# Head slots of a hybrid decoder block: the scores of a coming step are issued before the output projection's tile, not behind it

## The chip, the cores and the metric

One NeuronCore of a Trainium2 chip runs the whole kernel. The metric is the device time of one execution in microseconds (us), taken as the median of several runs. Everything is computed in 32-bit floating point; a matrix product is made of three matmuls on operands split into a high and a low part (hi x hi, lo x hi, hi x lo).

## What is computed

One layer of a decoder block over 512 tokens of width 1024: a projection that feeds an RG-LRU group and an attention group of 8 heads, an output projection of both groups together, a gated MLP with a short convolution, and a gated per-layer embedding. The part that matters here, cut from the reference:

```
proj = u @ w_in[i]
x_lru, g_lru, q, k, v = jnp.split(proj, split_at, axis=-1)
...
y_lru = rglru(...) * jax.nn.gelu(g_lru)
y_att = moba_attention(q, k, v, slopes)
h = h + jnp.concatenate([y_lru, y_att], axis=-1) @ w_out[i]
```

With 512 tokens there are two key blocks of 256 and the top-3 choice takes every past block, so each head is causal attention with a distance penalty: scores, softmax, probabilities times values. The matrix `w_out` has a half for the LRU rows and a half for the attention rows.

## The kernel before, in words

Each engine has its own hand-written, in-order list of instructions; semaphores tie them. TensorE (PE) does all matmuls, VectorE (DVE) and ScalarE (ACT) the element-wise work, GpSimd (POOL) mostly the low parts of weights. Weights stream in chunks of 128 x 1024 through a ring of four buffers.

The change lies in the stretch where the heads are worked. Three things are woven there on PE:

- **scores(st)**, one for each of 8 steps (lines 1151 to 1169): 12 matmuls on 64 rows (10 rows of the timeline, since two kinds are merged there), which write the banks 4, 5 and 6 of PSUM. These three banks exist once, so from step 1 on line 1155 has PE wait until all four parts of `logits(st-1)` have been read out of them by DVE (`logit_ok`).
- **turn_probs(h)** (lines 1171 to 1185): 10 transposes of the probabilities of head h into banks 0 to 2; then **values(h-1)** (lines 1187 to 1200): 8 matmuls into bank 7. In head 0 there are no values yet.
- **out_lru(h)** (lines 1202 to 1219): 12 matmuls, one of the eight output tiles of the LRU half of `w_out`. They are recorded under the lines 1040 to 1042 of the helper `three`. From h = 2 on they write bank 3, so they wait for the tile before to have been added (`part_ok`).

Ahead of the head loop PE issues `scores(0), out_lru(0), scores(1), out_lru(1), scores(2), out_lru(2)`. Then slot h of the loop is `turn_probs(h)`, `values(h-1)`, a projection tile, `scores(h+3)`. The projection tile is `out_lru(h+3)` in the slots 0 to 4; in the slots 5 to 7, where there are no scores left to issue, it is a part of the attention half (`out_att`).

The other two engines have slots of their own:

- DVE, slot h (lines 922 to 934): `add_lru(h+2)` (line 888, waits for the end of `out_lru(h+2)`), `logits(h+2)` (line 867, four parts, waits for `scores(h+2)`), the low parts of the turned probabilities of h (`prTlo`, line 929), `add_values(h-1)` (line 920), `normalise(h+2)` (lines 874 and 880, waits for the exponentials).
- ACT, slot h (lines 564 to 577): the high parts of the turned probabilities (`prThi`, line 569), `move_values(h-1)` (line 553, waits for `values(h-1)`), `exps(h+2)` (line 527, each part waits for its logits), in even slots `hi_att`, and `top_scale(h+2)` (line 536, waits for the reciprocals of `normalise`).

`turn_probs(h)` waits for the probabilities of both steps of its pair of heads: in an even slot, h = 2, 4, 6, that is the `top_scale(h+1)` which ACT issued in the slot before.

POOL splits the chunks of the attention half of `w_out` (lines 349 to 364) between the slots; each waits for `chunk_done`, which the odd tiles of `out_lru` raise.

Of the kernel before, what the change touches and what calls it, by code (L numbers as in the profile page):

```python
# [80 lines left out]
def score_order():  # L81

    halves = (((3, 4, 0), (0, 6, 0)), ((1, 6, P), (2, 5, 0)))
    order = []
    for half, tiles in enumerate(halves):
        start = 0
        for i, b, c0 in tiles:
            for term in range(3):
                order.append((start, half, term, i, b, c0))
                start += (i + 1) * P  # L90
    return [step[1:] for step in sorted(order)]


STEPS = 2 * PAIRS
# [17 lines left out]
def build(nc, x, x_t, p_t, lead_in, weights, vectors, gates, out):  # L112
    with ExitStack() as ctx:
# [80 lines left out]
        def parts_upto(st):  # L194

            return sum(len(parts(i)) for i in range(st))
# [177 lines left out]
        def _(act):  # L374
# [147 lines left out]
            def exps(st):  # L522

                for n, (e, i, _, _) in enumerate(parts(st)):
                    v = prob[(2 * (st // 2) + e) % 4][:, S_OFF[i]:S_OFF[i] + (i + 1) * P]
                    act.wait_ge(logit_ok, parts_upto(st) + n + 1)
                    nc.scalar.activation(v, v, ACT.Exp, bias=sm[:, st % 2, n:n + 1], scale=-1.0,
                                         accum_out=sm[:, st % 2, 10 + n:11 + n]).then_inc(exp_ok, 1)

            def top_scale(st):  # L530

                act.wait_ge(rinv_ok, st + 1)
                for n, (e, i, _, _) in enumerate(parts(st)):
                    if i >= TT - 2:
                        v = prob[(2 * (st // 2) + e) % 4][:, S_OFF[i]:S_OFF[i] + (i + 1) * P]
                        nc.scalar.activation(v, v, ACT.Copy, scale=sm[:, st % 2, 15 + n:16 + n]).then_inc(top_ok, 1)
# [27 lines left out]
            for h in range(HEADS):  # L564
                for part, (c0, b, w, _) in enumerate(TURNED):
                    act.wait_ge(pt_done, 3 * h + part + 1)
                    if h >= 2 and part == 0:
                        act.wait_ge(pv_done, h - 1)
                    nc.scalar.activation(prThi[h % 2][:, c0:c0 + w], bank[b][:, 0:w], ACT.Copy).then_inc(prT_hi, 1)
                if h:  # L570
                    move_values(h - 1)
                if h + 2 < STEPS:
                    exps(h + 2)
                if h and h % 2 == 0:
                    hi_att(h // 2 - 1)
                if h + 2 < STEPS:
                    top_scale(h + 2)
# [457 lines left out]
        def _(pe):  # L1035
# [115 lines left out]
            def scores(st):  # L1151

                p = st // 2
                if st:
                    pe.wait_ge(logit_ok, parts_upto(st))
                    pe.wait_ge(qkT_lo, PAIRS + p + 1)
                for half, term, i, b, c0 in score_order():
                    if st == 0 and term == 0:
                        pe.wait_ge(qkT_lo, PAIRS + b - 3)
                    e = half if st % 2 == 0 else 1 - half  # L1160
                    r, w = slice(DH * e, DH * (e + 1)), (i + 1) * P
                    q = (qkThi, qkTlo, qkThi)[term][0][r, p, i * P:w]
                    k = (qkThi, qkThi, qkTlo)[term][1][r, p, 0:w]
                    if i == 0 and term == 0:
                        pe.wait_ge(s_mid, st + 1)
                    last = mm(bank[b][:, c0:c0 + w], q, k, start=term == 0, stop=term == 2)  # L1166
                    if i == 1 and term == 2:
                        last.then_inc(s_mid, 1)
                last.then_inc(s_done, 1)

            def turn_probs(h):

                pe.wait_ge(prob_ok, 4 * (h // 2 + 1))
                pe.wait_ge(top_ok, 4 * (h // 2 + 1))
                if h:
                    pe.wait_ge(prT_lo, 3 * h)
                else:
                    pe.wait_ge(part_ok, 1)
                for c0, b, _, key_tiles in TURNED:
                    for kt in key_tiles:  # L1180
                        for i in range(kt, TT):
                            src = prob[h % 4][:, S_OFF[i] + kt * P:S_OFF[i] + (kt + 1) * P]
                            at_ = PT_OFF[kt] - c0 + (i - kt) * P
                            last = nc.tensor.transpose(bank[b][:, at_:at_ + P], src, ident[:, :])  # L1184
                    last.then_inc(pt_done, 1)

            def values(h):

                pe.wait_ge(prT_lo, 3 * (h + 1))
                if h:  # L1190
                    pe.wait_ge(att_ok, h)
                else:
                    pe.wait_ge(part_ok, 2)
                for kt in range(TT):
                    w = T - kt * P
                    v = vs[:, kt, h, :]
                    for n, src in enumerate((prThi[h % 2], prTlo[h % 2])):
                        last = mm(bank[PV_BANK][:, kt * P:T], v, src[:, PT_OFF[kt]:PT_OFF[kt] + w],  # L1198
                                  start=kt == 0 and n == 0, stop=kt == TT - 1 and n == 1)
                last.then_inc(pv_done, 1)  # L1200

            def out_lru(h):

                c, s = C_OL + h // 2, h // 2
                pe.wait_ge(w_lo, c - (RING - 1))
                pe.wait_ge(y_lo, LT)
                if h == 0:
                    pe.wait_ge(v_lo, 1)
                elif h == 1:
                    pe.wait_ge(qkT_lo, 2 * PAIRS)  # L1210
                elif h == 2:
                    pe.wait_ge(v_lo, TT)
                else:
                    pe.wait_ge(part_ok, h)
                for k in range(LT):
                    w = slice(k * 2 * P + (h % 2) * P, k * 2 * P + (h % 2 + 1) * P)
                    last = three(bank[FILL_BANK[h]][:, :], whi[s][:, w], wlo[s][:, w], mixhi[:, k, :], mixlo[:, k, :],
                                 k == 0, k == LT - 1)
                last.then_inc((half_done, chunk_done)[h % 2], 1)

            def out_att(s, tiles):

                pe.wait_ge(w_lo, C_OA + s - (RING - 1))
                for k, half in sorted(((k, half) for k in tiles for half in range(2)), key=lambda o: (o[0] // 2, o[1])):
                    if k == 0 and (s, half) in ((0, 0), (0, 1), (2, 0), (3, 0)):

                        pe.wait_ge(*{(0, 0): (part_ok, KD), (0, 1): (logit_ok, 4 * HEADS), (2, 0): (prT_lo, 3 * HEADS),
                                     (3, 0): (att_ok, HEADS)}[s, half])
                    pe.wait_ge(att_lo, k + 1)
                    w = slice(k * 2 * P + half * P, k * 2 * P + (half + 1) * P)  # L1230
                    last = three(bank[OA_BANK[2 * s + half]][:, :], whi[s][:, w], wlo[s][:, w],
                                 mixhi[:, LT + k, :], mixlo[:, LT + k, :], k == 0, k == PAIRS - 1)
                if tiles[-1] == PAIRS - 1:
                    last.then_inc(chunk_done, 1)
# [5 lines left out]
            for h in range(HEADS):  # L1240
                turn_probs(h)
                if h:
                    values(h - 1)
                if h + 3 < KD:
                    out_lru(h + 3)
                elif h == 5:
                    out_att(0, (0, 1))
                    out_att(1, (0,))
                elif h == 6:
                    out_att(1, (1,))  # L1250
                else:
                    out_att(0, (2,))
                    out_att(1, (2,))
                if h + 3 < STEPS:
                    scores(h + 3)
            values(HEADS - 1)
            out_att(2, (0, 1, 2))
            out_att(0, (3,))
# [139 lines left out]
```

## Times and profile before

| what | value |
|---|---|
| median of 3 runs | 656.53 us |
| lowest and highest of them | 656.22 and 656.76 us |
| the profiled execution's own time | 654.96 us |
| its span, first to last instruction | 653.2 us |
| mean granted clock of TensorE | 0.999 |
| PE busy (matmuls) | 646.2 us, 99% of the span |
| DVE busy | 354.2 us |
| ACT busy | 292.9 us |
| POOL busy | 326.8 us |

How to read it: the profile is one execution; times in the trace count from its first instruction. A timeline row gives the start, the time from there to the end of the last instruction of the row, the engine, the line, the operation, the tiles, how many instructions are merged in it, and in brackets how long the engine had been idle before it and what ended that. Matmuls are pipelined, so rows of PE overlap, and the distance between two starts says more than a duration. The same holds for rows of DVE and ACT, which overlap by some 0.07 us to 0.1 us. "issue" as a releaser means that the profile saw no event that ended the idle time.

### The profile page before, as it was taken

How to read it: one execution, taken by the hardware profiler on the slowest of the kernel's cores; microseconds unless marked ns; L12 is line 12 of the kernel's file. 1: busy time of each engine (PE TensorE's matmuls, PEld its weight loads, DVE VectorE, ACT ScalarE, POOL GpSimd, SP SyncE). 2: the span in 40 equal slices, each digit the busy share in tenths (PEclk: the TensorE clock that was granted, in tenths of full speed). 3: DMA queues.
4: the chain of work that ended last, by engine and by line, in shares of the span. 5: the costliest groups of instructions: out<-in, count | busy, mean ns of one | idle time of the engine just before them, and what ended most of it. 6: DMA issues, size and time to landing. Idle time of an engine off the chain costs nothing.

```text
span 653.2 us, 8651 instructions
## 1 busy us (share of the span) xinstructions
PE 646.2 (99%) x2980; PEld 535.0 (82%) x2980; DVE 354.2 (54%) x491; ACT 292.9 (45%) x445; POOL 326.8 (50%) x239
## 2 busy tenths in 40 slices
PE   8999999999999999999999999999999999999997
PEld 7788888887888888888888888888888888888886
DVE  4583699977649676555555555555422222222464
ACT  6668653778736454333333333333322222223521
POOL 6673433742207377555555555555544444444430
PEclk9999999999999999999999999999999999999999
DMA  8732221210403233222222222222322222222211
GB/s 319 276 125 91 97 96 65 96 34 1 162 1 125 70 100 126 96 96 96 96 96 96 96 96 96 96 96 96 102 97 96 99 95 97 96 98 97 75 64 50
DMA packets 20039, 65.41 MB, mean 100 GB/s; under 512 B 2224, under 2 KB 2864, under 8 KB 20016
## 3 DMA queue, kind: packets, MB, share of 16 engines
q1 hardware_dynamic: 19872, 64.97, 29.1%
q8 instruction: 14, 0.23, 0.1%
q10 hardware_dynamic: 144, 0.14, 0.1%
q14 instruction: 9, 0.07, 0.0%
HBM read 63.00 MB, written 2.10 MB: 100 GB/s over the span
## 4 chain that ended last, share of the span: by engine, by line
PE 98%; DMA 1%; DVE 0%; ACT 0%; issue 0%; DVEq 0%
PE bank L1040 30%; PE bank L1042 30%; PE bank L1041 30%; PE bank L1166 2%; PE bank L1198 2%; PE bank L1184 1%; PE bank L1078 1%; PE bank L1086 1%; PE bank L1081 1%; DMA lead<-in_lead_in 1%; PE bank L1136 1%; PE bank L1331 0%; PE bank L1277 0%; PE bank L1104 0%; ACT uhi L394 0%
## 5 line engine op out<-in xcount | busy, mean ns | idle before, releaser
L324 POOL TENSOR_TENSOR wlo<-raw,whi 128x512 fp32r<-128x512 f32 x106 | 142.9, 1348 | 262.9 <-ACT whi L382 262.5
L382 ACT ACTIVATE whi<-raw 128x1024 fp32r<-128x1024 f32 x102 | 107.6, 1058 | 226.1 <-PE bank L1042 226.0
L1040 PE MATMUL bank<-uhi,whi 128*128 128x512 f32 (+1 forms) x496 | 192.6, 388 | 0.0
L1042 PE MATMUL bank<-uhi,wlo 128*128 128x512 f32 (+1 forms) x496 | 191.4, 386 | 0.0
L1041 PE MATMUL bank<-ulo,whi 128*128 128x512 f32 (+1 forms) x496 | 191.4, 386 | 0.0
L325 POOL TENSOR_TENSOR wlo<-raw,whi 128x512 fp32r<-128x512 f32 x106 | 164.3, 1550 | 0.0
L1040 PEld LDWEIGHTS bank<-uhi,whi 128*128 128x128 f32 x496 | 93.2, 188 | 19.6 <-issue 0.7
L1041 PEld LDWEIGHTS bank<-ulo,whi 128*128 128x128 f32 x496 | 93.2, 188 | 19.5 <-issue 0.7
L1042 PEld LDWEIGHTS bank<-uhi,wlo 128*128 128x128 f32 x496 | 93.2, 188 | 18.6
L974 DVE SCALAR_TENSOR_TENSOR tmp<-tmp,vec 128x511 f32<-128x511 f32 (+1 forms) x48 | 63.4, 1320 | 27.9 <-ACT tmp L614 24.8
L1042 PE MATMUL bank<-acthi,wlo 128*128 128x512 f32 x192 | 74.7, 389 | 0.0
L1041 PE MATMUL bank<-actlo,whi 128*128 128x512 f32 x192 | 74.7, 389 | 0.0
L1040 PE MATMUL bank<-acthi,whi 128*128 128x512 f32 x192 | 74.7, 389 | 0.0
L992 DVE TENSOR_TENSOR res<-res,bank 128x512 f32 x8 | 5.5, 687 | 92.3 <-PE bank L1042 92.3
L1040 PEld LDWEIGHTS bank<-acthi,whi 128*128 128x128 f32 x192 | 36.0, 188 | 7.5
L1042 PEld LDWEIGHTS bank<-acthi,wlo 128*128 128x128 f32 x192 | 36.0, 188 | 7.4
L1041 PEld LDWEIGHTS bank<-actlo,whi 128*128 128x128 f32 x192 | 36.0, 188 | 7.4
L981 DVE TENSOR_TENSOR tmp<-tmp 128x512 f32<-128x512 f32 x24 | 27.0, 1124 | 22.3 <-ACT tmp L619 22.0
L1040 PE MATMUL bank<-whi,uhi 128*128 128x512 f32 x96 | 37.5, 391 | 0.0
L1042 PE MATMUL bank<-whi,ulo 128*128 128x512 f32 x96 | 37.4, 389 | 0.0
L1041 PE MATMUL bank<-wlo,uhi 128*128 128x512 f32 x96 | 37.4, 389 | 0.0
L983 DVE TENSOR_TENSOR actlo<-tmp,acthi 128x512 f32 (+1 forms) x24 | 19.0, 792 | 21.3 <-ACT acthi L623 21.3
(190 smaller groups left out, 823.8 us busy)
## 6 DMA issues: line engine op xcount, KB each, us to landing
raw<-in_weights SPq DMA_DIRECT2D x106, 512.0 KB, 3.3
res<-in_x_t SPq DMA_DIRECT2D x8, 256.0 KB, 5.4
xtok<-in_x SPq DMA_DIRECT2D x4, 512.0 KB, 8.1
raw<-in_weights SPq DMA_DIRECT2D x7, 256.0 KB, 6.4
out<-fin SPq DMA_DIRECT2D x7, 256.0 KB, 2.0
gw<-in_gates SPq DMA_DIRECT2D x1, 512.0 KB, 11.2
ptok<-in_p_t SPq DMA_DIRECT2D x1, 512.0 KB, 3.6
out<-fin SPq DMA_DIRECT2D x2, 128.0 KB, 1.8
```

What stands on the lines that cost most here:

```text
L324: nc.gpsimd.tensor_tensor(wlo[s][:, 0:CW // 2], raw[s][:, 0:CW // 2], whi[s][:, 0:CW // 2].bitcast(F32), ALU.subtract)
L325: nc.gpsimd.tensor_tensor(wlo[s][:, CW // 2:CW], raw[s][:, CW // 2:CW], whi[s][:, CW // 2:CW].bitcast(F32), ALU.subtract).then_inc(w_lo, 1)
L382: nc.scalar.activation(whi[s][:, :], raw[s][:, :], ACT.Copy).then_inc(w_hi, 1)
L974: V.scalar_tensor_tensor(y[:, k:T], g[:, 0:T - k], vec[:, bass.ds(f + (V_FCW + (2 - k) * FT), 1)], y[:, k:T], ALU.mult, ALU.add).then_inc( ...
L981: V.tensor_tensor(y, g, y, ALU.mult).then_inc(f_prod, 1)
L983: V.tensor_tensor(actlo[:, f, :], y, acthi[:, f, :].bitcast(F32), ALU.subtract).then_inc(act_lo, 1)
L1040: mm(o, ahi, bhi, start=start, stop=False)
L1041: mm(o, ahi, blo, start=False, stop=False)
L1042: return mm(o, alo, bhi, start=False, stop=stop)
L1078: mm(bank[m][:, :], whi[s][:, w[m]], uhi[:, k, :], start=k == 0, stop=False)
L1166: last = mm(bank[b][:, c0:c0 + w], q, k, start=term == 0, stop=term == 2)
L1198: last = mm(bank[PV_BANK][:, kt * P:T], v, src[:, PT_OFF[kt]:PT_OFF[kt] + w], start=kt == 0 and n == 0, stop=kt == TT - 1 and n == 1)
```

## The change

In each of the slots 0 to 4, `scores(h+3)` moves on PE from behind `out_lru(h+3)` to ahead of it. No instruction is added or removed, no wait is changed, and the lists of DVE, ACT, POOL and SyncE stay as they are. The loop ahead of the slots (steps 0 to 2) keeps its order, and the slots 5 to 7 issue no scores.

```
@@ -1241,6 +1241,8 @@
                 turn_probs(h)
                 if h:
                     values(h - 1)
+                if h + 3 < STEPS:
+                    scores(h + 3)
                 if h + 3 < KD:
                     out_lru(h + 3)
                 elif h == 5:
@@ -1251,8 +1253,6 @@
                 else:
                     out_att(0, (2,))
                     out_att(1, (2,))
-                if h + 3 < STEPS:
-                    scores(h + 3)
             values(HEADS - 1)
```

## Rows read from the trace of the kernel before

**Rows 1.** The page: busy time of the engines, granted clock, chain that ended last.

```profile
PE 646.2 (99%) x2980; PEld 535.0 (82%) x2980; DVE 354.2 (54%) x491; ACT 292.9 (45%) x445; POOL 326.8 (50%) x239
...
PEclk9999999999999999999999999999999999999999
...
PE 98%; DMA 1%; DVE 0%; ACT 0%; issue 0%; DVEq 0%
```

**Rows 2.** Timeline of PE, slot 0 (start us, us, engine, line, operation, tiles).

```profile
137.60 0.40 PE L1042 MATMUL bank<-mixhi,wlo 128*128 128x512 f32 x1
137.84 1.26 PE L1184 MATMUL bank<-ident,prob 128*128 128x128 f32 x10
138.88 0.47 PE L1040 MATMUL bank<-mixhi,whi 128*128 128x512 f32 x1
...
141.48 0.39 PE L1042 MATMUL bank<-mixhi,wlo 128*128 128x512 f32 x1
141.80 0.50 PE L1166 MATMUL bank<-kThi,qThi 64*128 64x512 f32 x2
...
143.07 1.31 PE L1184 MATMUL bank<-ident,prob 128*128 128x128 f32 x10
```

**Rows 3.** Timeline of PE, slot 1, from the values to the scores.

```profile
144.14 0.48 PE L1198 MATMUL bank<-prThi,vs 128*128 128x512 f32 x1
...
145.44 0.45 PE L1040 MATMUL bank<-mixhi,whi 128*128 128x512 f32 x1
...
148.02 0.39 PE L1042 MATMUL bank<-mixhi,wlo 128*128 128x512 f32 x1
148.34 0.49 PE L1166 MATMUL bank<-kThi,qThi 64*128 64x512 f32 x2
```

**Rows 4.** Timeline of PE: the transposes that open the slots 2 to 6.

```profile
149.99 1.28 PE L1184 MATMUL bank<-ident,prob 128*128 128x128 f32 x10 [0.31 <-issue]
...
156.52 1.31 PE L1184 MATMUL bank<-ident,prob 128*128 128x128 f32 x10
...
163.44 1.28 PE L1184 MATMUL bank<-ident,prob 128*128 128x128 f32 x10 [0.32 <-issue]
...
169.95 1.31 PE L1184 MATMUL bank<-ident,prob 128*128 128x128 f32 x10
...
176.88 1.28 PE L1184 MATMUL bank<-ident,prob 128*128 128x128 f32 x10 [0.23 <-issue]
```

**Rows 5.** Timeline of DVE, slot 0: the added tile and the logits.

```profile
138.04 0.69 DVE L888 TENSOR_TENSOR res<-res,bank 128x512 f32<-128x512 f32 x1 [2.86 <-PE bank L1042]
138.65 0.68 DVE L867 CUSTOM_DVE_ANT_0 prob<-bank,dist 128x512 f32<-128x512 f32 x1
...
140.08 0.28 DVE L867 CUSTOM_DVE_ANT_0 prob<-bank,dist 128x128 f32<-128x128 f32 x1
140.29 0.08 DVE L867 DVE_READ_ACCUMULATOR2_ANT sm<- 128x1 f32 x1
```

**Rows 6.** Timeline of PE: scores of step 2 and the projection tile behind them.

```profile
133.71 0.49 PE L1166 MATMUL bank<-kThi,qThi 64*128 64x512 f32 x2
...
134.98 0.50 PE L1040 MATMUL bank<-mixhi,whi 128*128 128x512 f32 x1
```

**Rows 7.** Timeline of ACT, slot 1: the moved values, the first exponential, the scaling.

```profile
145.64 0.60 ACT L553 ACTIVATE tmp<-bank 64x512 f32<-64x512 f32 x1 [0.51 <-PE bank L1198]
146.14 0.71 ACT L527 ACTIVATE prob<-prob,sm 128x512 f32<-128x512 f32 x1
...
148.66 1.23 ACT L536 ACTIVATE prob<-prob,sm 128x512 f32<-128x512 f32 x2 [0.24 <-DVE sm L874]
```

**Rows 8.** Timeline of DVE, slot 1: low parts of the turned probabilities, the reciprocals.

```profile
144.95 1.61 DVE L929 TENSOR_TENSOR prTlo<-bank,prThi 128x512 fp32r<-128x512 f32 x3
...
148.45 0.18 DVE L874 RECIPROCAL sm<-sm 128x4 f32<-128x4 f32 x1 [1.30 <-ACT prob L527]
```

**Rows 9.** Timeline of POOL: the second attention chunk of `w_out`.

```profile
142.86 1.04 POOL L352 CAST whi<-raw 128x1024 fp32r<-128x1024 f32 x1 [3.97 <-DVE prob L880]
```

## Prediction: the chances of a swap on a full engine

> **What bounds the kernel now.** I read the page first: TensorE is busy for 99% of the span at its full granted clock (the 2.4 GHz level), and the chain that ended last is 98% PE [rows 1]. So the time is PE's list of matmuls plus its idle gaps. A swap on PE leaves the list as it is, and can only make or remove gaps. Next I read PE's timeline through the slots for the brackets: ahead of the transposes of the slots 2, 4 and 6 PE idles 0.31, 0.32 and 0.23 us [rows 4]; the slots 0, 1, 3 and 5 open without a gap. There is thus some 0.9 us to win in the heads at the very most, and any new wait costs its full length. The swap shortens the time between two instructions that depend on each other through DVE, so the third view is DVE's timeline, which shows when the logits leave the score banks.
>
> **The dependence.** scores(h+3) waits until all four parts of logits(h+2) are read. On DVE logits(h+2) stand behind add_lru(h+2), which waits for the end of out_lru(h+2). Before, out_lru(h+2) ran ahead of scores(h+2): the tile was added while the scores ran, and from scores(h+2) to scores(h+3) PE had the transposes, the values and a whole tile to do. After, out_lru(h+2) is the last thing in PE's slot, so add_lru starts only when the next slot opens, the logits follow it, and PE has only transposes and values (in slot 0 only transposes) to cover both.
>
> **Slot 0, the main term.** Nothing ahead of it is changed: scores(2), out_lru(2) and the transposes at 137.84 stay [rows 2, 6]. DVE is already in the new pattern here: add_lru(2) starts at 138.04, the logits at 138.65, and their last part ends at 140.29 + 0.08 = 140.37 [rows 5]. The transposes take 138.88 - 137.84 = 1.04 us to the next matmul [rows 2]; scores start 0.32 us behind the last matmul of a tile where transposes start 0.24 us behind it (148.02 to 148.34, 137.60 to 137.84), 0.08 more, so free scores(3) would start at 138.96 [rows 2, 3]. How long PE takes from the release to the first matmul isn't shown for DVE as releaser. The nearest row: ACT's scaling ends at 148.66 + 1.23 = 149.89 and the transposes that wait for it start at 149.99, 0.10 us [rows 4, 7]. The other end is DVE starting 0.04 us after PE's last matmul ended (137.60 + 0.40 to 138.04) [rows 2, 5]; upwards I allow 0.3, three times the row. I take 0.10 as it has PE as the waiter. So scores(3) start at 140.47: a gap of 1.51 us. Behind them: scores to tile 134.98 - 133.71 = 1.27, tile to transposes 137.84 - 134.98 = 2.86 [rows 2, 6]. Slot 1 opens at 140.47 + 1.27 + 2.86 = 144.60 in place of 143.07: **+1.53 us** (+1.47 to +1.73).
>
> **Slots 1 and 3.** Call t the start of the slot's transposes. DVE repeats slot 0: logits done at t + 140.37 - 137.84 = t + 2.53, scores may start at t + 2.63. PE free: transposes 1.07 (143.07 to 144.14), values 1.30 (144.14 to 145.44), 0.08 for the change to scores: t + 2.45 [rows 2, 3]. A new gap of 0.18. Without other waits the slot would take 2.63 + 1.27 + 2.86 = 6.76 us. But the slot's end waits for top_scale: from 143.07 to 149.99 it took 6.92, and slot 3 6.92 too (156.52 to 163.44) [rows 2, 4]. That chain runs on ACT from the values: moved at 145.64, exponentials at 146.14 = t + 3.07, reciprocals, scaling [rows 7, 8]. Its logits were wanted at t + 3.07 and are there at t + 2.53, so it is neither later nor earlier, and 6.92 hides 6.76. **+0** each (0 to +0.18).
>
> **Slots 2 and 4.** They open 0.16 later than the tile ahead of them ended (6.92 - 6.76), and so DVE, which had started with that tile, has the logits out at t + 2.37 and PE may go at t + 2.47; free it would go at t + 2.45. The slot takes 2.47 + 1.27 + 2.86 = 6.60, in place of 6.53 (149.99 to 156.52) and 6.51 (163.44 to 169.95) [rows 4]. **+0.07 and +0.09** (0 to +0.25 each).
>
> **Slot 5 and on.** No scores are issued. add_lru(7) and the logits come some 0.4 us later against the transposes than before, but the exponentials again wait for the values, t + 3.07 against t + 2.53; the slot stays at 176.88 - 169.95 = 6.93 us [rows 4]. I count 0.
>
> **What is moved along.** prTlo(h) on DVE went ahead from 144.95 = t + 1.88 and now follows the logits at t + 2.45; it ends at about t + 4.05, adding the values at t + 4.7, and the reciprocals wait for ACT until 148.45 = t + 5.38 anyway [rows 8], so ACT and the next slot see none of it. The projection's ends move, and with them the DVE add (free by then) and POOL: the cast of the second attention chunk waited for the probabilities until 142.86 [rows 9] and will now wait for the end of out_lru(3) at about 144.8; with its two splits (2.5 us more by its own pace) it is ready before 149, and the first attention tile isn't issued before slot 5, after 170 [rows 4]. The swap passes no DMA issue and no other queue. After the heads everything is shifted as a block, and I find no gap of PE there that could take the shift in.
>
> **Sum.** 1.53 + 0.07 + 0.09 = +1.69 us. The profiled execution took 654.96, so its counterpart would be 656.65; the median of the runs lies 1.57 above the profiled time, and I set the sum on the median: 656.53 + 1.69 = **658.2 us**, +0.26%. What a measurement of this kernel can tell from no change is about 0.2%, 1.31 us, so the forecast lies just past that line, and the lower half of its error crosses it.
>
> **The rivals.**
>
> *The gap is taken in by the waits that are there.* If the three top_scale waits ended at fixed times, set by ACT alone, the later PE would find them over: 149.99 less the free start of slot 2, which is 148.34 + 1.27 = 149.61, gives 0.38 for each of the first two and 0.23 to 0.4 for the third, some 1.1 us [rows 3, 4, 6]. The result would be 1.69 - 1.1 = +0.6, 657.1 us, not slower by over 0.2%. It decides if ACT's exponentials could start ahead of the moved values. Against it: ACT's bracket at 145.64 says that it waited for PE's values [rows 7], so the chain moves with PE. Chance 0.09.
>
> *Every slot pays.* If the release of the scores, or the later prTlo, reaches ACT's chain as well, the four slots 1 to 4 pay 0.18 each on top of what they have, without the cover of the 6.92: 1.53 + 4 x 0.18 + 0.16 = +2.4, 658.9 us. For it: a part of DVE's slack, t + 4.7 against t + 5.38, is used up. Against: 0.7 us of it is left. Chance 0.09.
>
> *The swap brings what its order suggests.* Scores that end sooner could give earlier logits, exponentials and scaling, and two of the waits (0.38 each) would vanish: without the gap in slot 0 -0.8, 655.7. It needs DVE's logits to be free of the tile; they are not, by DVE's own order. Chance 0.02, half of it past 0.2% for what I don't see.
>
> *The clock falls.* PE has a gap of 1.5 us in slot 0 where it had none, and if the granted clock then drops to 1.2 GHz for about a slot, its 6.5 us of matmuls take twice the time: +1.7 + 6.5, 664.7 us. Against it: the page shows the clock at its top in every slice, also in the first, in which PE began with nothing done [rows 1]. Chance 0.03. The Trainium skill ("TensorE: Matmul & The Clock Gate", "The HAM clock gate") says that idle time gates the clock down to half and that renewed activity releases it; the trace of before has no gap of such length inside the stream of matmuls that could show it, so the rule stays as this rival and no more.
>
> **How the numbers follow.** The forecast's own case has 0.77: 0.69 of it lands above +1.31 us, 0.08 below, as the runs alone spread by 0.5 us. Faster: 0.01 (half of the third rival). Same: 0.08 + 0.09 + 0.01 = 0.18. Slower: 0.69 + 0.09 + 0.03 = 0.81. The range: down to +0.9 (gap of 1.47, no term behind it, half the spread of the runs and a rest), 657.4, up to +2.7, 659.2, which takes in "every slot pays"; left out are the first rival, the third and the clock, and a tail of the forecast, about 2 in 10.
>
> **What the profile after would show.** Right: an idle bracket of about 1.3 to 1.5 us ahead of the scores in slot 0, ended by DVE's logits; DVE's add_lru in the slots 1 to 4 starting 0.2 us after the transposes, the logits right behind; the slots 1, 3 and 5 still 6.9 us long, the slots 2 and 4 6.6; granted clock unchanged. Wrong: slot 0 no longer than 5.3 us, slots 1 and 3 over 7.0, brackets ahead of slots 2, 4 and 6 that are gone, or a clock below the top behind slot 0.

## The result, and the profile after

| | before | changed |
|---|---|---|
| median | 656.09 us (10 runs, 655.43 to 656.76) | 657.54 us (10 runs, 657.08 to 658.55) |
| the profiled execution | 654.96 us | 657.29 us |
| its span | 653.2 us | 655.5 us |
| start of the transposes of slot 0 | 137.84 us | 138.57 us |
| PE busy | 646.2 us | 646.2 us |

The ratio of the times is 1.0022, 95% interval 1.0014 to 1.0031: 1.45 us slower, between 0.9 and 2.0. The value on record was 658.2 us, +1.69 us. Of the 0.66 us between 658.2 and 657.54, 0.44 us is the median of before that the sum was set on (656.53, three runs, where ten give 656.09). One run of the kernel before, of the 81 that stood beside the experiments, took 810.75 us at a mean granted clock of 0.753; it is left out of all comparisons.

PE did the same work in both, so the loss is idle time. The waits of PE in the profile of the changed kernel (who waited for whom: us in total, times, longest):

```profile
...
PE bank L1166 <- DVE sm L867: 1.3, 1, 1.3
PE bank L1040 <- DVE ulo L675: 1.3, 1, 1.3
...
PE bank L1184 <- issue: 0.2, 1, 0.2
```

The first line shown is the predicted gap, ahead of the scores (L1166), ended by DVE's logits (L867). The second lies at 23.29 us, 115 us ahead of the heads: PE waits there for low parts that DVE computes (L675). The profile of before has no such line, so the stretch ahead of the change differs from execution to execution. In the thirteen profiles of this study the transposes of slot 0 start between 137.84 and 139.63 us, whatever the kernel. The two spans differ by 2.3 us; 0.73 of it lies ahead of the slots, so spans must not be compared, slots must. From the transposes of slot 0 to those of slot 6 the old kernel takes 39.04 us and the new one 40.57, **+1.53**; from there to the end 476.32 and 476.36.

Timeline of PE in the changed kernel, slots 0 and 1, which answers to [rows 2, 3]:

```profile
138.57 1.25 PE L1184 MATMUL bank<-ident,prob 128*128 128x128 f32 x10
141.16 0.49 PE L1166 MATMUL bank<-kThi,qThi 64*128 64x512 f32 x2 [1.33 <-DVE sm L867]
...
145.32 1.25 PE L1184 MATMUL bank<-ident,prob 128*128 128x128 f32 x10
...
147.91 0.49 PE L1166 MATMUL bank<-kThi,qThi 64*128 64x512 f32 x2
```

Timeline of DVE, the same stretch, which answers to [rows 5]:

```profile
138.77 0.69 DVE L888 TENSOR_TENSOR res<-res,bank 128x512 f32<-128x512 f32 x1 [2.86 <-PE bank L1042]
139.38 0.68 DVE L867 CUSTOM_DVE_ANT_0 prob<-bank,dist 128x512 f32<-128x512 f32 x1
...
141.02 0.08 DVE L867 DVE_READ_ACCUMULATOR2_ANT sm<- 128x1 f32 x1
...
145.52 0.69 DVE L888 TENSOR_TENSOR res<-res,bank 128x512 f32<-128x512 f32 x1 [1.99 <-PE bank L1042]
...
147.77 0.08 DVE L867 DVE_READ_ACCUMULATOR2_ANT sm<- 128x1 f32 x1
```

Read them together. In slot 0 the tile is added at 138.77, the logits end at 141.02 + 0.08 = 141.10, and the scores start at 141.16. In slot 1 DVE has itself become idle for 1.99 us until the tile is done (before, it started its add in that slot at 142.71 without a bracket, ahead of the transposes at 143.07), adds it at 145.52, and its logits end at 147.85, 0.06 us ahead of the scores at 147.91: the pair runs hand in hand, as in slot 0, but values now cover most of it. What is left of the gap shows in the distance from the last matmul of the values to the scores, in slot 1 and in slot 2:

```profile
147.53 0.27 PE L1198 MATMUL bank<-prTlo,vs 128*128 128x128 f32 x1
147.91 0.49 PE L1166 MATMUL bank<-kThi,qThi 64*128 64x512 f32 x2
...
154.45 0.27 PE L1198 MATMUL bank<-prTlo,vs 128*128 128x128 f32 x1
154.65 0.49 PE L1166 MATMUL bank<-kThi,qThi 64*128 64x512 f32 x2
```

In slot 1 it is 0.38 us, in slot 2 it is 0.20; the 0.18 between them is the wait of slot 1, as long as predicted. The starts of the transposes of the later slots, which answer to [rows 4]:

```profile
152.20 1.28 PE L1184 MATMUL bank<-ident,prob 128*128 128x128 f32 x10
...
158.82 1.26 PE L1184 MATMUL bank<-ident,prob 128*128 128x128 f32 x10
...
165.69 1.28 PE L1184 MATMUL bank<-ident,prob 128*128 128x128 f32 x10
...
172.28 1.25 PE L1184 MATMUL bank<-ident,prob 128*128 128x128 f32 x10
...
179.14 1.28 PE L1184 MATMUL bank<-ident,prob 128*128 128x128 f32 x10 [0.23 <-issue]
```

The brackets ahead of slots 2 and 4 are gone, but the slots ahead of them are not shorter for it: the gap has moved to the scores in the middle of the slot, and the slot still ends where ACT's scaling ends. Behind the last matmul of the tile (151.80) the transposes come after 0.40 us, where they come after 0.23 us when nothing holds them (145.09 to 145.32). ACT in slot 1, which answers to [rows 7]:

```profile
147.85 0.59 ACT L553 ACTIVATE tmp<-bank 64x512 f32<-64x512 f32 x1 [0.53 <-PE bank L1198]
148.34 0.71 ACT L527 ACTIVATE prob<-prob,sm 128x512 f32<-128x512 f32 x1
...
150.87 1.23 ACT L536 ACTIVATE prob<-prob,sm 128x512 f32<-128x512 f32 x2 [0.25 <-DVE sm L874]
```

The scaling ends at 150.87 + 1.23 = 152.10 and the transposes follow at 152.20, 0.10 behind as before.

### The profile page after: what moved, and what is told of

It reads as the page before. It is cut to its first block, busy times and chain, and to the rows that moved or that the text cites. A ratio compares the mean times of both kernels' runs of the same rounds, so it can differ in the third digit from the quotient of the medians.

```text
span 655.5 us, 8651 instructions
## 1 busy us (share of the span) xinstructions
PE 646.2 (99%) x2980; PEld 534.8 (82%) x2980; DVE 354.9 (54%) x491; ACT 293.0 (45%) x445; POOL 326.7 (50%) x239
## 4 chain that ended last, share of the span: by engine, by line
PE 95%; DVE 2%; DMA 1%; SPq 1%; ACT 1%; issue 0%; DVEq 0%
PE bank L1040 30%; PE bank L1042 30%; PE bank L1041 30%; PE bank L1166 2%; PE bank L1198 1%; DMA res<-in_x_t 1%; PE bank L1184 1%; DVE prob L867 1%; PE bank L1136 1%; DVE small L704 0%; SPq L253 0%; DVE ulo L675 0%; DVE res L888 0%; ACT uhi L394 0%; SPq L260 0%
```

## The experiments

All kernels ran beside runs of the kernel before. Lengths of slots are distances between the starts of the transposes in the profile, in us; they are free of the differing start of the kernel, and so resolve a tenth where the medians don't.

| kernel | slot 0 | 1 | 2 | 3 | 4 | 5 | sum | ratio of times (95%) |
|---|---|---|---|---|---|---|---|---|
| before | 5.23 | 6.92 | 6.53 | 6.92 | 6.51 | 6.93 | 39.04 | |
| changed | 6.75 | 6.88 | 6.62 | 6.87 | 6.59 | 6.86 | 40.57 | 1.0022 (1.0014 to 1.0031) |
| swap in slot 0 alone | 6.73 | 6.87 | 6.53 | 6.92 | 6.51 | 6.93 | 40.49 | 1.0021 (1.0012 to 1.0031) |
| swap in slots 1 to 4 | 5.25 | 6.92 | 6.54 | 6.87 | 6.57 | 6.88 | 39.03 | 1.0003 (0.9994 to 1.0012) |
| swap, logits first on DVE | 5.32 | 6.88 | 6.57 | 6.87 | 6.54 | 6.87 | 39.05 | 0.9996 (0.9987 to 1.0005) |
| logits first, no swap | 5.21 | 6.93 | 6.59 | 6.93 | 6.64 | 6.93 | 39.23 | 1.0007 (0.9998 to 1.0016) |
| one op added, no swap | 5.22 | 6.93 | 6.50 | 6.93 | 6.51 | 6.93 | 39.02 | 1.0003 (0.9994 to 1.0012) |
| two ops added, no swap | 5.52 | 6.91 | 6.51 | 6.92 | 6.52 | 6.92 | 39.30 | 1.0004 (0.9994 to 1.0014) |
| swap, small op added | 7.09 | 6.88 | 6.58 | 6.87 | 6.58 | 6.87 | 40.87 | 1.0032 (1.0020 to 1.0045) |
| swap, one op added | 8.89 | 6.88 | 6.57 | 6.87 | 6.58 | 6.87 | 42.66 | 1.0056 (1.0043 to 1.0069) |
| swap, two ops added | 10.81 | 6.87 | 6.61 | 6.87 | 6.58 | 6.87 | 44.61 | 1.0078 (1.0062 to 1.0095) |
| exponentials early, no swap | 5.25 | 6.54 | 6.53 | 6.55 | 6.53 | 6.54 | 37.94 | 0.9979 (0.9971 to 0.9988) |
| all three orders changed | 5.33 | 6.56 | 6.54 | 6.56 | 6.56 | 6.49 | 38.04 | 0.9990 (0.9981 to 0.9998) |

**Which slots pay?** The swap was cut in two.

```
# slot 0 alone: (0,); its complement: (1, 2, 3, 4)
+                if h in (0,):
+                    scores(h + 3)
                 if h + 3 < KD:
                     out_lru(h + 3)
...
-                if h + 3 < STEPS:
+                if h + 3 < STEPS and h not in (0,):
                     scores(h + 3)
```

> The kernel before with the swap made in slot 0 alone; the slots 1 to 4 keep tile, then scores. Theory (the tile's add stands ahead of the logits on DVE, and slot 0 has no values to cover both): nearly the whole loss sits here, a bracket of 1.3 to 1.5 us ahead of the scores of slot 0, slot 0 6.75 us long in place of 5.23, all other slots as before; +1.5 us against the kernel before. Rival (each swapped slot costs its share, by the change of order on PE itself): a fifth of the loss, +0.3 us.

> The kernel before with the swap made in the slots 1 to 4 and not in slot 0. Theory: slot 0 as before (5.23 us); slots 1, 3 and 5 unchanged within 0.1 us since their end is set by ACT's scaling, slots 2 and 4 longer by 0.07 to 0.09: between 0 and +0.2 us in all, no change that can be measured. Rival (each slot costs its share): four fifths of the loss, +1.2 us.

Measured: slot 0 alone gives 657.70 us against 655.85 and a slot 0 of 6.73 us; the other four give 656.01 and a sum of slots that is 0.01 below before. The whole loss is in slot 0, where there are no values to cover the logits; slot 1 is 0.05 shorter. The rival of equal shares falls. In the second kernel slots 2 and 4 are 0.01 and 0.06 longer, as forecast or less, and slots 3 and 5 give 0.05 each back.

**What makes PE wait: the swap, or DVE's order?** The same swap, with the logits ahead of the tile's add:

```
@@ DVE, slot h
-                if h + 2 < KD:
-                    add_lru(h + 2)
                 if h + 2 < STEPS:
                     logits(h + 2)
+                if h + 2 < KD:
+                    add_lru(h + 2)
```

> The changed kernel with one more edit, on DVE: in each slot the logits stand ahead of the tile's add. Theory: the scores' wait is for logits that no longer wait for the tile; in slot 0 the logits are out near turn start minus 1 us, the bracket ahead of the scores of slot 0 is gone, slot 0 is back at 5.2 to 5.3 us, slots 1, 3, 5 stay at 6.9 and slots 2 and 4 at 6.55: equal to the kernel before within 0.2 us. Rival (scores next to the values or transposes cost PE by themselves): still +1 us or more. A second rival (earlier logits bring earlier exponentials): up to 0.8 us faster than before; theory says no, as ACT's exponentials stand behind the moved values.

Measured: 655.88 us, no difference from before, slot 0 back at 5.32. DVE's timeline of this kernel around its slot 0:

```profile
136.80 0.69 DVE L867 CUSTOM_DVE_ANT_0 prob<-bank,dist 128x512 f32<-128x512 f32 x1
...
138.45 0.08 DVE L867 DVE_READ_ACCUMULATOR2_ANT sm<- 128x1 f32 x1
139.75 0.69 DVE L888 TENSOR_TENSOR res<-res,bank 128x512 f32<-128x512 f32 x1 [1.22 <-PE bank L1042]
```

and PE's:

```profile
139.55 1.26 PE L1184 MATMUL bank<-ident,prob 128*128 128x128 f32 x10
140.73 0.50 PE L1166 MATMUL bank<-kThi,qThi 64*128 64x512 f32 x2
```

The logits are out at 138.53, a microsecond ahead of the transposes, and the scores have no bracket. So the wait came from the tile's add in front of the logits, not from the scores' new neighbours on PE. A rest of 0.09 us in slot 0 (5.32 against 5.23) is the order on PE itself: from the transposes to the scores it takes 1.18 us (139.55 to 140.73) with nothing waiting, where it took 1.04 to the tile. It also shows that the earlier scores bring nothing of their own.

The DVE edit alone, without the swap:

> The kernel before with the DVE edit alone: logits ahead of the tile's add, no swap on PE. It splits the pair: theory expects no change, within 0.2 us, as the logits then start when the scores end, at the same time as now (0.6 us earlier in the odd slots at most) and nobody waits for them sooner. If DVE's order by itself gains or costs, it shows here.

Measured: 656.52 us, ratio 1.0007, not clear of 1; but the sum of slots is 0.19 longer, all in slots 2 and 4; the expectation had named no cause for that. In the old order the tile comes before the scores on PE, and it waits for the add of the tile before it (they share bank 3). In slot 1 of this kernel, the add on DVE, then the last row of values and the first of the tile on PE:

```profile
146.40 0.68 DVE L888 TENSOR_TENSOR res<-res,bank 128x512 f32<-128x512 f32 x1
...
146.91 0.28 PE L1198 MATMUL bank<-prTlo,vs 128*128 128x128 f32 x1
147.23 0.47 PE L1040 MATMUL bank<-mixhi,whi 128*128 128x512 f32 x1
```

They are 0.32 apart where nobody waits at 0.11 (145.33 to 145.44 in the kernel before); the add had ended at 147.08. In the odd slots ACT's scaling hides this; in the slots 2 and 4 the two rows are 0.19 and 0.20 apart (153.81 to 154.00 in slot 2, with the add's end at 153.86), and there it shows. Each order on DVE goes with one on PE; crossed, either way, PE waits.

**How much cover was there?** An addition of 128x512 into a tile that nobody reads was put on DVE in slot 0, between the tile's add and the logits:

```
                 if h + 2 < KD:
                     add_lru(h + 2)
+                if h == 0:
+                    V.tensor_tensor(tmp[:, 1, :], res[:, 0, :], res[:, 1, :], ALU.add)
                 if h + 2 < STEPS:
                     logits(h + 2)
```

> The kernel before with one added operation on DVE in slot 0, between the tile's add and the logits: a 128x512 addition into a tile that nobody reads, about 0.6 us. It measures the cover of the old order. Theory: logits(2) done at 141.0 in place of 140.4 us of the trace, scores(3) not asked for before 141.8: hidden, +0.0 us (under 0.2). Rival (DVE is on the path in both orders): +0.6 us.

> The changed kernel with the same added operation of about 0.6 us ahead of the logits in slot 0. Theory: in the new order PE waits for exactly this chain, so it comes through at full length: the bracket ahead of the scores of slot 0 grows from 1.33 to about 1.95 us, +0.6 us over the changed kernel, +2.1 us over the kernel before. Rival (the gap in slot 0 is set by something other than DVE's chain): no more than the changed kernel's +1.45.

Measured without the swap: 655.97 against 655.89 us, slot 0 5.22: hidden. With two such operations:

> The kernel before with the same two added operations of 128x512 ahead of the logits of slot 0, some 1.35 us. It measures where the cover of the old order ends. In the trace of before logits(2) are done at 140.37 and scores(3) start at 141.80, with 0.06 to 0.10 us from release to start: cover about 1.35 us. Theory: the two operations are hidden or leave a bracket of under 0.2 us ahead of the scores, slot 0 5.2 to 5.4 us, +0.0 to +0.2 us, clock at its top. Rival (added DVE work costs PE time in any order): +0.7 us or more.

Measured: 656.17 against 656.10 us. PE's timeline:

```profile
143.50 0.50 PE L1169 MATMUL bank<-kThi,qThi 64*128 64x512 f32 x2
145.08 1.28 PE L1187 MATMUL bank<-ident,prob 128*128 128x128 f32 x10 [0.23 <-DVE prTlo L932]
```

The scores start 3.94 us after the transposes (139.56), where the kernel before has 3.96 [rows 2]. The logits came 1.32 us later and ended at 143.40, 0.10 us ahead of the scores: covered, and the cover is used up. The slot is 5.52 long nevertheless, 0.1 above the expected end. `turn_probs(h)` also waits for the low parts of head h-1 (`prT_lo`), and these, queued behind the logits, end at 144.93 and are late for the transposes. That is the next thing in line in the old order.

With the swap the one operation gave a surprise: 659.45 us, slot 0 8.89, 2.14 us over the changed kernel where 0.6 was expected. PE's bracket was near the 1.95 expected; the added operation moved the logits by 0.71 us, not 0.6:

```profile
142.09 0.71 PE L1168 MATMUL bank<-kThi,qThi 64*128 64x512 f32 x2 [2.04 <-DVE sm L867]
```

The rest is the clock. The windows of this kernel (stretch, us; busy us of PE, PEld, DVE, ACT, POOL; granted clock of TensorE; DMA share and GB/s):

```profile
139.80:142.00 2.20, 0.26 (x3) 0.02 (x1) 2.20 (x10) 1.96 (x6) 0.05 (x1) 1.00 0.00 0
142.00:143.00 1.00, 0.91 (x6) 0.91 (x8) 1.00 (x4) 1.00 (x5) 0.00 (x0) 0.61 0.00 0
143.00:144.00 1.00, 1.00 (x9) 0.86 (x5) 0.96 (x5) 0.65 (x3) 0.00 (x0) 0.50 0.00 0
144.00:145.00 1.00, 1.00 (x3) 0.79 (x4) 0.24 (x2) 0.92 (x2) 0.00 (x0) 0.50 0.00 0
145.00:146.00 1.00, 1.00 (x4) 0.76 (x4) 0.00 (x0) 0.00 (x0) 0.00 (x0) 0.69 0.00 0
146.00:147.00 1.00, 1.00 (x7) 0.78 (x5) 0.00 (x0) 0.00 (x0) 0.00 (x0) 1.00 0.00 0
```

The clock is at its top through the idle stretch and falls at about 142.2, as PE takes up work again; it is back at about 145.6 (both worked out from the windows of 0.61 and 0.69, with 0.50 and 1.00 as the two levels). In between it is 0.50, the 1.2 GHz level, and matmuls of 512 columns start 0.42 us apart (145.15 and 145.57) in place of 0.23. The changed kernel, with its bracket of 1.33, keeps 1.00 in every such window. Two more doses on the changed kernel, one of 160 columns and one of two operations of 512:

> The changed kernel with a smaller added operation on DVE ahead of the logits of slot 0 (160 columns, about 0.25 us by the 0.28 and 0.42 us that the parts of 128 and 256 columns of the logits take). It asks where the extra 1.5 us of the 0.6 us operation came from. Theory (a gap on PE costs its own length, and past some length the granted clock falls behind it): bracket 1.33 + 0.25 = 1.6 us, slot 0 near 7.0 us, clock at its top or, if it falls, slot 0 near 8.3. Rival (the added operation slows PE by itself, by DVE's traffic): the slot is longer than the gap explains with the clock at its top.

> The changed kernel with two added operations of 128x512 ahead of the logits of slot 0, some 1.35 us. Theory (gap plus one fall of the clock): bracket about 2.7 to 2.8 us, granted clock at half (1.2 GHz) for about the same 3 us as with one operation, slot 0 9.5 to 9.7 us, +4.3 us against the kernel before: 0.7 us more than with one. Rival (the loss grows with DVE's added work, about 3.5 times its length as with one): slot 0 11 us, +6 us.

Measured with the small operation: bracket 1.68, slot 0 7.09 and the clock at its top in the profiled execution, 657.88 us in the median of ten runs. Three of them took 659.5 to 660.3 us at a mean clock of 0.996 to 0.997; the other seven lay at 657.0 to 658.4 with 0.998 to 1.000. That the clock fell in those three is read from these two numbers alone, as none of them was the profiled one. With two operations: 661.40 us, slot 0 10.81. The size was missed again (9.5 to 9.7 were expected), since the low level started sooner and lasted longer:

```profile
141.50:142.00 0.50, 0.00 (x0) 0.00 (x0) 0.50 (x5) 0.50 (x3) 0.00 (x0) 0.72 0.00 0
142.00:143.00 1.00, 0.75 (x5) 0.75 (x7) 1.00 (x4) 1.00 (x5) 0.00 (x0) 0.50 0.00 0
...
147.00:148.00 1.00, 1.00 (x4) 0.71 (x3) 0.00 (x0) 0.00 (x0) 0.00 (x0) 0.50 0.00 0
148.00:149.00 1.00, 1.00 (x5) 0.82 (x4) 0.00 (x0) 0.00 (x0) 0.00 (x0) 0.72 0.00 0
```

The scores start at 142.25, so here the clock fell, at about 141.7, while PE was still idle. The bracket (2.65) accounts for 1.3 us more than in the changed kernel, the half clock from about 141.7 to 148.4 for 2.7. The rival's number, 11 us, came nearer to the 10.81 than the theory's. Its mechanism is not borne out all the same: without the swap the same two operations leave the slot at 5.52, and with it the loss beyond the bracket goes with the windows at 0.50.

**What do the odd slots end on?** The prediction counted them at 6.92 by a chain on ACT that starts with PE's values. If so, another order on ACT and DVE cuts it, with PE untouched:

```
@@ ACT, odd slots with scores left (1, 3, 5); the others as before
-                move_values(h - 1); exps(h + 2); top_scale(h + 2)
+                exps(h + 2); top_scale(h + 2); move_values(h - 1)
@@ DVE, the same slots
-                add_values(h - 1); normalise(h + 2)
+                normalise(h + 2); add_values(h - 1)
```

> The kernel before, PE untouched, with another order on ACT and DVE in the odd slots 1, 3 and 5: exponentials and scaling ahead of the moved values on ACT, normalise ahead of adding the values on DVE. It tests what the end of the odd slots hangs on. Theory: the transposes of the slots 2, 4 and 6 wait for the scaling, whose chain starts with PE's values by ACT's order only; with it cut, exponentials start behind the turned probabilities, at about t + 2.0 in place of t + 3.07, the scaling ends near t + 5.8, the three brackets (0.31, 0.32, 0.23) vanish and the odd slots take 6.55: -1.1 us against the kernel before. Rival (the chain hangs on the logits or on PE): no change; or the later moved values delay the values of the next slot: slower.

Measured: 654.78 against 655.89 us, ratio 0.9979 (0.9971 to 0.9988), the three brackets gone, each odd slot 0.38 shorter, the sum of slots -1.10. ACT in slot 1 of this kernel (transposes of slot 1 at 144.69, of slot 2 at 151.23):

```profile
146.62 0.74 ACT L527 ACTIVATE prob<-prob,sm 128x512 f32<-128x512 f32 x1
...
149.15 1.23 ACT L536 ACTIVATE prob<-prob,sm 128x512 f32<-128x512 f32 x2 [0.24 <-DVE sm L877]
150.40 0.59 ACT L553 ACTIVATE tmp<-bank 64x512 f32<-64x512 f32 x1
```

The scaling ends at 150.38, 0.85 us ahead of the transposes of slot 2 (151.23). This version is faster than the kernel before and the changed one. With the swap and the logits first on top of it:

> Everything together: the swap on PE, logits ahead of the tile's add on DVE, and exponentials ahead of the moved values in the odd slots. Theory: the swap neither gains nor costs once DVE's order doesn't tie the logits to the tile, so it equals the same edit without the swap: -1.1 us against the kernel before (-0.9 to -1.2). Rival (earlier scores help once ACT is free to use them): faster than that by 0.3 us or more.

Measured: 655.36 us, ratio 0.9990 (0.9981 to 0.9998), sum of slots 38.04: by the slots -1.00 against the kernel before, by the medians -0.53, where -1.1 was expected. The slots say 0.10 worse than without the swap (0.08 in slot 0), the medians 0.58; the intervals overlap, and where the rest of that difference lies wasn't settled. That the swap would help once ACT is free is not borne out by either.

## Why the prediction was right, point by point

**Bound and dependence.** Right as put: PE's list unchanged (646.2 us busy in both), one new wait on the logits, and the logits tied to the tile by DVE's order. The two kernels with the logits first show the last point, which before was only read from the code. One bound was too low: "some 0.9 us to win in the heads at the very most" added up the brackets (0.86), while the waits are 0.38 us each by the starts of the rows, as the rival on the waits had it, and the kernel with early exponentials won 1.10 in the slots.

**Slot 0, +1.53.** Measured 6.75 - 5.23 = +1.52, and 6.73 with the swap there alone. Inside it, two small errors cancel. Release to first matmul was 0.06 us (141.10 to 141.16), not 0.10. From the scores to the next transposes it took 145.32 - 141.16 = 4.16 in place of 1.27 + 2.86 = 4.13. The gap itself was put at 1.51 from a free start of the scores 1.12 us behind the transposes; without a wait they start 1.18 behind (the kernel with the logits first), so 1.41 us of waiting and 0.09 us of the order on PE itself make up the 1.52 within their spread.

**Slots 1 and 3, +0 each.** Measured -0.04 and -0.05, slot 5 -0.07. The chain moves with PE's values, and these come sooner: transposes that follow a tile take 1.01 us to the first values (145.32 to 146.33), those that follow scores 1.07 [rows 2, 3]. The prediction had taken one price, 1.07, for both. The scores of slot 1 start at t + 2.59 (147.91 - 145.32), against t + 2.63.

**Slots 2 and 4, +0.07 and +0.09.** Measured +0.09 and +0.08, but the agreement to 0.02 is luck. With the same swap in the slots 1 to 4 alone they are +0.01 and +0.06, so one profile doesn't fix terms of this size. The wait that was forecast, 0.02 us, isn't there: in slot 2 the logits end at 154.55 and the scores follow the values at the 0.20 us above. What is longer is the tile: from its first matmul to the next transposes 2.90 us (155.92 to 158.82), against 2.83 in the kernel with the swap in the slots 1 to 4 alone. Why that distance varies stays open.

**The signs.** One was badly chosen: I had listed brackets gone from ahead of the slots 2, 4 and 6 as a sign of being wrong. Two are gone and the slots are as long as worked out. By my own numbers PE's slack ahead of them shrinks from 0.38 to 0.16 us with the gap of 0.18 in the middle of the slot, which is too little for a bracket to be listed. The length of the slot was the sign to name, not the place of its idle time.

**The sum.** +1.69 against +1.53 in the slots: the 0.16 is what the three odd slots gave back. The runs say +1.45 with an interval (0.9 to 2.0) that holds both. The mechanism and its price in the slots are shown by the runs; the hit in absolute time is narrower than it looks. The range, 657.4 to 659.2, was set on a median of before that was 0.44 too high, and 657.54 lies 0.14 above its lower end. The call "past +1.31 us" came out by the same 0.14, and that line lies inside the interval.

**What was moved along.** In slot 1 the low parts now start at 147.77 = t + 2.45, as worked out. POOL's cast of the second chunk, in answer to [rows 9]:

```profile
145.65 1.04 POOL L352 CAST whi<-raw 128x1024 fp32r<-128x1024 f32 x1 [6.02 <-PE bank L1042]
```

It waits for the tile, as foreseen, and costs nothing; its last split ends at 149.30, with the first attention tile after 172.28.

**The rivals.** "Taken in by the waits" and "every slot pays" are both out by the slot lengths. "Brings what its order suggests" is out by the swap with the logits first: nothing gained. "The clock falls" did not happen in the changed kernel (its ten runs have mean clocks of 0.998 to 1.000), but it was argued with the wrong row. The clock of the first slices says nothing of a gap within a running stream, and the doses show that another 0.35 us of gap brings the fall in three runs of ten and 0.7 us in five of six, by the mean clocks of the runs. Its price was too high as well: the fall cost 1.4 us behind a gap of 2.04 (8.89 - 6.75 less 0.71 of longer bracket) and 2.7 behind 2.65, not a slot's 6.5. The Trainium skill ("TensorE: Matmul & The Clock Gate", "The HAM clock gate") has idle time bring the half clock; the traces agree, with 0.50 granted behind both gaps.

## What to carry to other kernels

When an instruction is moved ahead on one engine, look up what the engine that answers it has queued in front of the answer: here the scores went first on PE but the tile's add stayed first on DVE, so what PE gained in order it lost in cover. Work out the cover slot by slot, as the one without its usual filler (slot 0, no values) can hold the whole loss. And where a full engine has small waits, the gain lies in the order of the engine that it waits for: another order on ACT and DVE brought 1.1 us, moving the scores brought none.

## What the runs showed of the hardware that was not expected

- A gap on PE of 1.33 us in the midst of dense matmuls left the granted clock at its top in the profile; 21 runs of two kernels with it had mean clocks of 0.998 to 1.000. At 1.68 us three of ten runs had a mean clock of 0.996 to 0.997, at 2.04 us five of six, at 2.65 us all four (0.993 to 0.997). Without such a gap 0.997 is rare: one of the other 80 runs of the kernel before (657.59 us), one of 11 of "logits first, no swap" (657.88) and one of 10 of "two ops added, no swap" (658.35). The loss grows from 1.52 us for a bracket of 1.33 to 5.58 us (10.81 - 5.23) for one of 2.65. All of these gaps follow on ten transposes; no run here has one behind other matmuls.
- How long after the release PE starts depends on the pair: scores 0.06 us after DVE's logits end (141.10 to 141.16, 147.85 to 147.91), transposes 0.10 us after ACT's scaling (152.10 to 152.20), but a tile 0.15 us after DVE's add (147.08 to 147.23, "logits first, no swap") and transposes 0.15 us after DVE's low parts (144.93 to 145.08, "two ops added, no swap").
- Ten transposes take 1.01 us to the first values behind a 128-row tile (145.32 to 146.33) and 1.07 behind 64-row scores. What follows counts too: behind a tile it takes 1.04 us to another tile and 1.18 to scores.
